# One decoder step on one core: the recurrent layer's x tiles before its gate tiles, and the samples' attention among the prompt's units

## What is computed

```python
def recurrent_block(xn, conv_buf, h0, w_in, conv_w, conv_b, wa, ba, wx, bx, lam, w_out):
    proj = xn @ w_in
    gate = gelu(proj[..., :D_RNN], approximate=True)
    xc, new_buf = causal_conv(proj[..., D_RNN:], conv_buf, conv_w, conv_b)
    h, h_last = rg_lru(xc, h0, wa, ba, wx, bx, lam)
    return (h * gate) @ w_out, new_buf, h_last

def rg_lru(x, h0, wa, ba, wx, bx, lam):
    r = sigmoid(block_diag(x, wa, ba));  i = sigmoid(block_diag(x, wx, bx))
    log_a = -RG_C * r * softplus(-lam);  a = exp(log_a)
    bterm = sqrt(-expm1(2.0 * log_a)) * i * x     # + a[:, 0] * h0 at the start
    # h[t] = a[t] * h[t-1] + bterm[t], along the tokens

def sink_softmax(s, mask, sink):
    m = maximum(max(where(mask, s, -inf)), sink)
    p = exp(s - m)
    return p / (sum(p) + exp(sink - m))
```

## Time and profile before

| what | value |
|---|---|
| median of three runs | 3308.62 us |
| the profiled execution | 3303.82 us, its span 3302.0 us |
| TensorE busy (PE) | 3073.0 us, 93% |
| VectorE busy (DVE) | 2525.9 us, 76% |
| POOL busy | 1824.0 us, 55% |
| ScalarE busy (ACT) | 1378.4 us, 42% |
| the chain that ended last | PE 71%, DVE 15%, DMA 8% |
| costliest lines of the chain | L1591 27%, L1539 23% (expert stages), L1471 11% |

### The profile page before, as it was taken

One profiled execution on the slowest core, in us unless ns is written; L12 is line 12 of the kernel. 1 busy time (PEld: TensorE's weight loads), 2 busy tenths in 40 slices (PEclk: granted clock), 3 DMA queues, 4 the chain that ended last, 5 costly groups with the idle time before them and its releaser, 6 DMA issues.

```text
span 3302.0 us, 46678 instructions
## 1 busy us (share of the span) xinstructions
PE 3073.0 (93%) x17202; PEld 2778.0 (84%) x17202; DVE 2525.9 (76%) x4955; ACT 1378.4 (42%) x2549; POOL 1824.0 (55%) x1160
## 2 busy tenths in 40 slices
PE   6969999899998999999888889999899999999997
PEld 5868999899998887778674689999899988877776
DVE  2775899976773999899567347999777739998987
ACT  2233334376764333333344122343666653333332
POOL 3533388787874445666130133688677843555662
PEclk9989999999999999999988799999899999999998
DMA  3212299899998999999130022799899989999993
GB/s 94 90 32 88 89 319 341 289 373 387 401 390 309 398 401 398 401 396 388 56 94 1 13 66 77 257 341 343 301 385 402 390 311 397 399 398 397 398 401 143
DMA packets 286578, 920.90 MB, mean 279 GB/s; under 512 B 27344, under 2 KB 77392, under 8 KB 282688
## 3 DMA queue, kind: packets, MB, share of 16 engines
q1 hardware_dynamic: 154336, 415.63, 34.9%
q0 software_dynamic: 111280, 404.77, 32.3%
q10 hardware_dynamic: 20736, 97.53, 7.3%
HBM read 817.34 MB, written 102.38 MB: 279 GB/s over the span
## 4 chain that ended last, share of the span: by engine, by line
PE 71%; DVE 15%; DMA 8%; POOL 2%; issue 1%; ACT 1%; SPq 1%; DVEq 0%; ACTq 0%; POOLq 0%
PE ps L1591 27%; PE ps L1539 23%; PE ps L1471 11%; PE ps L1571 5%; DMA sring<-s_dram 4%; DMA raw<-uT 2%; POOL low L559 1%; DVE xn L875 1%; DVE xl L868 1%; DMA raw<-v 1%; DMA rowsB<-u,pick 1%; DVE cand L1145 1%; PE ps L1681 1%; DVE cand L1152 1%; DVE slot L1158 1%
## 5 line engine op out<-in xcount | busy, mean ns | idle before, releaser
L693 ACT ACTIVATE high<-raw 128x1024 fp32r<-128x1024 f32 x512 | 542.4, 1059 | 961.1 <-PE ps L1591 647.1
L559 POOL TENSOR_TENSOR low<-raw,high 128x1024 fp32r<-128x1024 f32 x256 | 614.0, 2399 | 229.5 <-ACT high L693 225.7
L1539 PE MATMUL ps<-xh,high 128*128 128x384 f32 x2048 | 700.4, 342 | 11.5 <-POOL low L559 11.5
L1539 PE MATMUL ps<-xh,low 128*128 128x384 f32 x2048 | 688.4, 336 | 0.0
L1539 PE MATMUL ps<-xl,high 128*128 128x384 f32 x2048 | 687.2, 336 | 0.0
L1591 PE MATMUL ps<-high,hh 128*128 128x512 f32 x1536 | 486.6, 397 | 23.5 <-DVE low L1228 23.5
L1591 PE MATMUL ps<-low,hh 128*128 128x512 f32 x1536 | 482.9, 395 | 0.0
L1591 PE MATMUL ps<-high,hl 128*128 128x512 f32 x1536 | 481.5, 394 | 0.0
L550 POOL DMA_INDIRECT rowsB<-v,pick x192 | 294.8, 1536 | 276.9 <-DVE ps L1063 239.0
L550 POOL DMA_INDIRECT rowsA<-v,pick x192 | 300.3, 1564 | 213.4 <-DVE ps L1063 207.0
L1539 PEld LDWEIGHTS ps<-xh,high 128*128 128x128 f32 x2048 | 387.1, 189 | 15.4 <-POOL low L559 14.6
(11 more groups left out here) (280 smaller groups left out, 5130.7 us busy)
## 6 DMA issues: line engine op xcount, KB each, us to landing
raw<-uT SPq DMA_DIRECT2D x256, 512.0 KB, 7.0
raw<-v SPq DMA_DIRECT2D x256, 512.0 KB, 14.4
gate_dram<-gblk ACTq DMA_DIRECT2D x24, 2048.0 KB, 11.5
gt<-gate_dram SPq DMA_DIRECT2D x32, 1536.0 KB, 20.9
s_dram<-sring ACTq DMA_DIRECT2D x120, 384.0 KB, 7.2
sring<-s_dram SPq DMA_DIRECT2D x120, 384.0 KB, 15.0
raw<-wts SPq DMA_DIRECT2D x72, 512.0 KB, 3.7
rowsB<-u,pick POOLq DMA_INDIRECT x192, 8.1
```

The costliest lines, as they stand in the source:

```text
L559: pool.tensor_tensor(low[:, m % 4], raw[:, m % 4], high[:, (m + 2) % 3].bitcast(F32), ALU.subtract).then_inc(sem("lo_ready"), 1)
L693: act.activation(high[:, (m + 2) % 3], tile_raw(m), ACT.Copy).then_inc(sem("hi_ready"), 1)
L1539: ins = pe.matmul(ps[:, m % 2, 0:DN], w[:, c], x[:, c, 0:DN], start=(c == 0 and k == 0), stop=(c == NC - 1 and k == 2))
```

## The change

Five things change.

- The first norm's sum of squares goes over all eight chunks on TensorE; VectorE's five additions there fall away. A dummy root (of `eps`) is put ahead of the first, third, fourth and fifth norms' roots on ScalarE.
- The x tiles come first. Then follow gate tile 0, the first block-diagonal product, gate tile 1, the second product, and gate tiles 2 to 7. The products get their own pair of PSUM banks each (4 to 7). Gate tiles 0 to 4 are only copied at first and go through gelu after the roots, tiles 5 to 7 go through gelu when they are done.
- So xh and xl must live longer: `ig` and `dec` move out of their place, `dec` to that of `xpre`, and the output weights' place is that of `xc` (two of them instead of four, `OUTS`), loaded after a new semaphore `xc_used`. `outputs` sums two tiles chunk by chunk, six follow as ordinary tiles. `lag` becomes 5.
- The units have four places for the weights (`PRS`), and one PSUM bank for the result instead of two.
- The samples' scores are items 4 and 5 in the queue of score items; the maximum comes in unit 2, exponentials in 3, the sum in 4, the turns in 5 and 6 in the units' banks, one value product per unit from 8 on, the copies in unit 12 and at the end.

The diff, cut to what the prediction speaks of:

```diff
-W_IN, W_A, W_X, W_OUT, W_PQ0, W_K, W_Q, W_O, W_PQ1, W_N = 0, 16, 17, 18, 26, 42, 44, 52, 60, 76
+W_IN, W_A, W_X, W_OUT, W_PQ0, W_K, W_Q, W_O, W_PQ1, W_N = 0, 9, 11, 18, 26, 42, 44, 52, 60, 76
+W_GATE = (8, 10, 12, 13, 14, 15, 16, 17)
+D_GATE = (8, 17, 26, 27, 28, 29, 30, 31)
+LATE_GATES = 5
-OUTS = 4
+OUTS = 2
+S_ITEM = 4
+EXP_AT, SUM_AT_UNIT, TURN_AT, MIX_AT, KEEP_AT = 3, 4, 5, 8, 12
+PRS = 4
...
             def load_weights(lo, hi):
...
+                    if w == W_GATE[5]:
+                        spq.wait_ge(sem("xc_used"), 1)
+                        for f in range(OUTS):
+                            spq.dma_start(outR[:, f], wts[W_OUT + f]).then_inc(sem("out_loaded"), 16)
+                    if w - 2 in (W_A, W_X):
+                        spq.wait_ge(sem("tile_done"), tiles_made(w - 2))
...
+            def gate_output(f):
+                if f < LATE_GATES:
+                    pool.wait_ge(sem("gate_ready"), f + 1)
+                else:
+                    pool.wait_ge(sem("d_free"), D_GATE[f] + 1)
+                pool.wait_ge(sem("scanned"), f + 1)
+                pool.tensor_tensor(xn[:, f], rg[:, f], gate[:, f], ALU.mult).then_inc(sem("x_whole"), 1)
...
             def square(s):
+                if s > 1:
+                    act.activation(eps[:, 1:2], eps[:, 0:1], ACT.Sqrt)
...
                 for k, (d0, dst, bias) in enumerate(((D_A, rg, P_BA), (D_X, ig, P_BX))):
+                    take_gate(k)
...
+                take_gate(2)
                 act.wait_ge(sem("dec_ready"), NC)
...
+                take_gate(3)
...
+                take_gate(4)
+                for f in range(LATE_GATES):
+                    gelu_gate(f)
+                for f in range(LATE_GATES, NC):
+                    gelu_late_gate(f)
                 split_x(X_OUT)
...
             def rg_lru():
                 dve.wait_ge(sem("params_loaded"), 16)
-                for c in range(1, SUMMED + 1):
-                    add_squares(0, c)
...
-                lag = 4
+                lag = 5
...
-                    if u >= 2:
-                        dve.wait_ge(sem("pturn"), u - 1)
+                    if u >= PRS:
+                        dve.wait_ge(sem("pturn"), u - PRS + 1)
...
+                for u in range(UNITS):
+                    normalise(u)
+                    for k in items_due(u):
+                        item(k)
+                    if u:
+                        keep(u - 1)
+                    if u == EXP_AT - 1:
+                        sample_max()
+                    if u == SUM_AT_UNIT:
+                        sample_normalise()
+                    if u == KEEP_AT:
+                        sample_keep(0)
+                keep(UNITS - 1)
+                sample_keep(1)
...
+            def inputs():
+                project(W_IN, D_IN, NC, X_IN)
+                for f in range(NC):
+                    project_tile(W_GATE[f], D_GATE[f])
+                    if f < 2:
+                        rg_gates((W_A, W_X)[f], (D_A, D_X)[f])
...
+                for u in range(UNITS):
+                    for k in items_due(u):
+                        item(k)
+                    turn(u)
+                    if u:
+                        mix(u - 1)
+                    if u in (TURN_AT, TURN_AT + 1):
+                        sample_turn(u - TURN_AT, u)
+                    if u >= MIX_AT:
+                        sample_mix(u - MIX_AT)
+                mix(UNITS - 1)
```

More of the change, by code:

```diff
@@ L132, in turned_tile, with item_of, items_due @@
     return (n - KEPT) % KEYS
+UNITS = NQB * NKV
+S_ITEM = 4
+EXP_AT, SUM_AT_UNIT, TURN_AT, MIX_AT, KEEP_AT = 3, 4, 5, 8, 12
+PRS = 4
+def item_of(u):
+    return u + 2 * (u >= S_ITEM)
+def items_due(u):
+    return range(0 if u < 0 else item_of(u + 1) + 1, min(item_of(u + 2), UNITS + 1) + 1) if u >= 0 else range(2)
 def groups_of(m):
@@ L221, in decoder @@
         mark = base.take("mark", [P, 1])
-        eps = base.take("eps", [P, 1])
+        eps = base.take("eps", [P, 2])
         keepP = base.take("keepP", [P, NC, CW - 1])
@@ L367, in decoder @@
         ACC, SCS, TURN, IOTA = 6, 6, 6, 7
+        OUT, OUTS_B = 6, 7
         SUM, SUMS = 4, 7
@@ L499, in split_weights @@
                         pool.dma_start(vKeep, vc.rearrange("p b n -> b p n")[:, TS:WIN]).then_inc(sem("kept"), 16)
[L500 to L509, removed]
-                    if w == W_OUT + OUTS:
[L511 to L520, removed]
+                    if w in W_GATE[5:5 + OUTS]:
+                        out_split(w - W_GATE[5])
+                    if w == W_GATE[7]:
+                        gate_output(0)
+                    if w == W_OUT + OUTS:
+                        for f in range(1, NC):
+                            gate_output(f)
                     n = splits_made(w) - 1
@@ L622, in rg_lru @@
                 act.activation(sp[:, 2], sp[:, 1], ACT.Ln).then_inc(sem("softplus_step"), 1)
-                for f in range(NC):
-                    act.wait_ge(sem("tile_done"), D_IN + f + 1)
-                    act.activation(two(gate[:, f]), halves(dbank(f)), ACT.Gelu_apprx_tanh
-                                   ).then_inc(sem("d_free"), 1)
                 act.wait_ge(sem("pad_ready"), 1)
@@ L816, in attention @@
                 exps(1)
-                for u in range(NQB * NKV):
+                for u in range(UNITS):
                     act.wait_ge(sem("pturn"), u + 1)
@@ L1414, in attention, with sample_normalise @@
-                for g in range(GRP):
-                    e = g % 2
-                    for bb in range(2):
+                def sample_normalise():
+                    dve.wait_ge(sem("sexp"), 2)
+                    chain.did(dve.tensor_reduce(smS[:, 4], pss[:, :, :], X, ALU.add))
+                    chain.settle()
+                    chain.did(dve.tensor_tensor(smS[:, 4], smS[:, 4], smS[:, 3], ALU.add))
+                    chain.settle()
+                    chain.did(dve.reciprocal(smS[:, 5], smS[:, 4]))
+                    chain.settle()
+                    dve.tensor_tensor(pss[:, :, :], pss[:, :, :],
+                                      smS[:, 5].unsqueeze(2).broadcast_to([P, NB, WIN + TS]), ALU.mult
+                                      ).then_inc(sem("s_ready"), 1)
@@ L1417, in attention, with sample_keep @@
+                def sample_keep(bb):
+                    dve.wait_ge(sem("s_out"), bb + 1)
+                    for g in range(GRP):
+                        e = g % 2
                         ins = dve.tensor_copy(
@@ L1448, in sum_squares @@
                     pe.wait_ge(sem("ones_ready"), 1)
-                pe.wait_ge(sem("sq_added"), SUMMED * (SUM_AT[s] + 1))
-                for c in (0, NC - 2, NC - 1):
-                    if c:
+                    chunks = range(NC)
+                else:
+                    pe.wait_ge(sem("sq_added"), SUMMED * (SUM_AT[s] + 1))
+                    chunks = (0, NC - 2, NC - 1)
+                for c in chunks:
+                    if c or not s:
                         pe.wait_ge(sem("sq_ready"), SQ[s] + c + 1)
@@ L1729, in attention, with sample_turn @@
-                ins.then_inc(sem("sturn"), 1)
-                pe.wait_ge(sem("pssT_ready"), 1)
-                for b in range(NB):
+                def sample_turn(part, u):
+                    if part == 0:
+                        pe.wait_ge(sem("s_ready"), 1)
+                    pe.wait_ge(sem("prT_ready"), u + 1)
+                    for b in range(NB):
+                        o = ps[0:(P, TS)[part], 2 + b // 4, (b % 4) * P:(b % 4 + 1) * P]
+                        ins = pe.transpose(o, pss[:, b, (0, WIN)[part]:(WIN, WIN + TS)[part]], ident)
+                    ins.then_inc(sem("sturn"), 1)
```

333 lines of the change are left out of this document (173 added, 160 removed).

## The result

The changed kernel takes 3254.43 us (median of four runs, 3249.49 to 3261.32) beside 3309.49 before: ratio 0.9845, 95% interval 0.9828 to 0.9862. It is faster by 1.5%, clear of the noise and in the direction forecast, but by 55 us where the forecast had 72 (from the profiled execution) or 77 (from the median then shown). The median lies at the upper edge of the range, 3212 to 3256; the ratio applied to the median shown, 3308.62, gives 3257.3, just outside.

What follows compares the result with a forecast made beforehand. Most of the run is bound by TensorE in the untouched expert stages, so stretches where TensorE waits were targeted. 41.9 - 1.3 + 30.3 - 0.2 + 1.3 = 72.0 us off 3303.8 gives 3232, range 3212 to 3256.

Steps and rivals of the forecast that it cites:

- First norm: Start of the recurrent layer: with TensorE summing all eight squares, the root ends at 18.2 us, 12.1 earlier.
- The two gates: Recurrent layer, x tiles first: the second gate's products end at 109.5 us instead of 168.8, 59.3 earlier.
- Six gate tiles under the recurrence: Recurrent layer: tiles run beside the recurrence, end at 149.1 us; layer outputs end at 210.7 instead of 252.6, 41.9 earlier.
- part 1: Recurrent layer's first norm: TensorE sums all eight squares, VectorE adds none; root 12.1 us earlier, bounds 7.7 to near 15.
- POOL's queue (rival c): Recurrent layer: a gate product delays the last gate tile's split on POOL, some 10 us; total 3242 us; chance 7%.
- The recurrence as the bound (rival d): Layer 0: recurrence, not TensorE, sets its end whatever the order; only the attention gains; about 3272 us; chance 2%.
- The second root's load: Second norm, after the scans: the root must load its own table on the path, 1.3 us lost.
- The units: Layer 1's attention, first to sixteenth turn: no shorter, 110 us, TensorE the bound; ends 92 and 125.
- (a): Attention units: TensorE's clock rises with filled gaps, VectorE sets them at 98 us; total 3220 us; chance 15%.
- (b): Attention units: small products hold TensorE's clock at 0.65, units take 125 us; total 3247 us; chance 15%.
- The end of the attention: Layer 1, sixteenth turn to the output's first split: 9.5 us instead of 39.8, 30.3 won.
- Fourth norm: After layer 1's attention: a dummy root ahead hides the table load, 1.28 us on the chain before; 1.3 won.

## Why the prediction was wrong, by its own steps

- **First norm:** right, 17.7 for 18.2.
- **The two gates:** right, 111.1 for 109.5.
- **Six gate tiles under the recurrence, the step that failed.** "The six end at 149.1 ... VectorE waits for that in its sixth scan." I counted the six tiles' 38.4 us for TensorE, beside ScalarE's functions, and put what VectorE's squares and products and POOL's splits cost each other at nothing. Before, the squares and products ran while POOL was idle; the change puts six of POOL's splits on top of them and a seventh on the scans. They took 12.3 and 14.4 us, and the first scan began at 144.05 (130.28 without the subtractions). The last gate tile ended at 160.7: 1.6 late at the start, then 1.1 more than forecast for the fourth tile's weight, 3.7 and 0.2 of waits, and 4.9 for the lower clock behind waits. The first output chunk came at 164.5 instead of 151.2, the outputs at 224.1 instead of 210.7, below the gain that I had given as the layer's lower bound (28.4 against 30). The run without the subtractions gives 211.2, in part by luck, as said there. The pace was there to be seen: a low half of 1.98 beside POOL's product, which I used for a bound of the low halves alone, and, plainest, the five squares that part 1 takes away from VectorE. Before, they took 7.45 us beside two splits of POOL, where eight took 5.44 with POOL idle:

```profile
15.01 7.45 DVE L858 TENSOR_TENSOR xn<-xn 128x576 f32<-128x576 f32 x5 [15.01 <-DMA prm<-params]
```

```profile
16.15 1.37 POOL L535 CAST high<-raw 128x1024 fp32r<-128x1024 f32 x1 [11.81 <-DMA raw<-wts]
17.61 2.72 POOL L537 TENSOR_TENSOR low<-raw,high 128x1024 fp32r<-128x1024 f32 x1
```

- **POOL's queue (rival c):** its place was right, its mechanism not. The last gate tile waited 0.21 us for POOL's split; the queue mattered by what it did to VectorE.
- **The recurrence as the bound (rival d):** nearest in mechanism, at 2%. The chain did run through VectorE's recurrence to the layer's end, but its price was wrong: the layer still won 28.4 us.
- **The second root's load:** 1.28 us on the chain, as said; the root ended 4.5 behind the outputs instead of 3.7, so it cost 0.8, since part of it lay beside the last squares' sum.
- **The units:** 112.7 for 110, TensorE the bound, clock 0.80 between rivals (a) and (b), neither of which came. The nearness is partly luck: the forecast was 106 of work and 4 of waits for the samples' turns, the trace has 98.3 of work and 14.5 idle, 13.1 of it in seven waits for VectorE's division. The wait of unit 12 was not foreseen; I had looked at the turns' shared bank and not at who copies the samples' result out of theirs.
- **The end of the attention:** 10.4 for 9.5. **Fourth norm:** the load is hidden, worth 0.8 rather than 1.3; the other 1.4 of that stretch are the output tiles, 51.7 us instead of 53.2.
- **Not in the sum:** 5.7 us ahead of the third norm, at the lower clock; why it fell stays open.

In sum: 13.0 of the missing 18 lie in the recurrent layer (the subtractions alone were worth 12.9), 5.7 are the third norm's clock, 3.6 the attention; the other stages gave some 4 back.

## What to carry to other kernels

When work of POOL is moved beside work of VectorE, price VectorE's two-input instructions by POOL's and not by their own length: here one of them got through for each instruction of POOL, so a subtraction of 2.8 us on POOL held VectorE longer than making it itself, at 1.21. Where one engine's stage is to hide another's, price the pairs that have never run side by side in the old trace by the nearest pair that has; where two paths end almost together, plan for both. And where a result bank is halved, look for who copies it out, and what stands ahead of that copy in its queue.

## What the hardware showed that was not expected

- Taking 12.3 us off VectorE won 3.2 us; taking seven subtractions off POOL won 12.9.
- The same instructions behind the same 2.5 us wait ran at a granted clock of 1.00 or of 0.70 to 0.76, 15.4 or 19.5 to 21.2 us, by kernels that differ elsewhere; units of one and the same code took 111 to 118 us, the longest at a clock of 0.78, the shortest at 0.82.
- Filling TensorE's gaps in the units raised the granted clock little (0.78 to 0.80); in the four kernels in which the wait in unit 12 was gone as well it was 0.80, 0.81, 0.86 and 0.86.
